# Sixty-four-column products set among the gate/up products, and products behind the last expert, in an encoder layer kernel

## What is computed

```python
def expert_choice_ffn(h, w_router, w_gate, w_up, w_down):
    n = B * L
    cap = max(1, EC_FACTOR * n // N_EXPERTS)      # 64 of the prompt, 128 of the sample
    hf = h.reshape(n, D)
    aff = jax.nn.softmax((hf @ w_router).astype(jnp.float32), axis=-1)
    g, idx = lax.top_k(aff.T, cap)
    xe = hf[idx]
    hid = jax.nn.silu(jnp.einsum('ecd,edf->ecf', xe, w_gate)) * jnp.einsum('ecd,edf->ecf', xe, w_up)
    ye = jnp.einsum('ecf,efd->ecd', hid, w_down) * g[..., None].astype(h.dtype)
    y = jnp.zeros((n, D), h.dtype).at[idx.reshape(-1)].add(ye.reshape(-1, D))
```

## Time and profile before

| | before |
|---|---|
| median of 3 runs | 3176.76 us (3174.6, 3176.76, 3177.8) |
| span of the profiled execution, first to last instruction | 3174.2 us |
| mean granted TensorE clock | 0.995 |
| PE busy | 3117.6 us (98%), 19002 products |
| PEld busy | 2799.1 us (88%) |
| DVE busy | 2304.2 us (73%) |
| ACT busy | 1907.7 us (60%) |
| HBM read | 650.35 MB |

### The profile page before, as it was taken

The page is one execution under the profiler, slowest core; times in us unless marked ns, Lnnn a source line. Parts: engine busy times, 40 slices in busy tenths (PEclk is TensorE's granted clock), DMA queues, the critical chain, the costliest instruction groups (busy, mean ns, idle before and its releaser), DMA issues.

```text
span 3174.2 us, 49405 instructions
## 1 busy us (share of the span) xinstructions
PE 3117.6 (98%) x19002; PEld 2799.1 (88%) x19002; DVE 2304.2 (73%) x3555; ACT 1907.7 (60%) x3129; POOL 187.8 (6%) x191
## 2 busy tenths in 40 slices
PE   7999999998999999999999999999999999999998
PEld 5777766787999999999999999999999999999997
DVE  6789848458777767777777777777777776777775
ACT  6244478444666666656666666666666666665664
POOL 0000000001010101010101001010101010101000
PEclk9999999999999999999999999999999999999999
DMA  9321266437575747575766666675757574757562
GB/s 345 126 77 57 79 218 224 146 112 282 200 283 199 284 183 289 212 281 211 257 232 258 231 246 241 237 259 212 262 199 282 199 286 185 288 213 282 208 250 93
DMA packets 140941, 692.78 MB, mean 218 GB/s; under 512 B 11040, under 2 KB 48432, under 8 KB 116912
## 3 DMA queue, kind: packets, MB, share of 16 engines
q1 hardware_dynamic: 131680, 663.55, 56.1%
q0 software_dynamic: 8128, 25.17, 3.2%
q10 hardware_dynamic: 912, 1.00, 0.2%
HBM read 650.35 MB, written 39.34 MB: 217 GB/s over the span
## 4 chain that ended last, share of the span: by engine, by line
PE 76%; DVE 1%; DMA 0%; issue 0%; POOL 0%; ACT 0%; POOLq 0%; DVEq 0%
PE psG L1902 35%; PE psG L1904 16%; PE psY L1921 5%; PE psY L1924 5%; PE psY L1922 5%; PE psY L1923 5%; PE psY L1925 5%; DVE idxu L1362 0%; DVE affT L1365 0%; DVE vals L1359 0%; DMA xg<-xhat_d,iall 0%; PE psY L1840 0%; POOL out L1967 0%; DVE yp L2173 0%; DVE ye L2167 0%
## 5 line engine op out<-in xcount | busy, mean ns | idle before, releaser
L1902 PE MATMUL psG<-xe,w_gu_hi_part 128*128 128x384 f32 x5632 | 1617.2, 358 | 0.0
L1904 PE MATMUL psG<-xe,w_gu_lo_part 128*128 128x192 f32 x5632 | 1410.3, 250 | 0.0
L1904 PEld LDWEIGHTS psG<-xe,w_gu_lo_part 128*128 128x128 f32 x5632 | 1074.7, 191 | 13.1
L1902 PEld LDWEIGHTS psG<-xe,w_gu_hi_part 128*128 128x128 f32 x5632 | 1057.4, 188 | 13.8 <-DVE xe L2233 0.4
L2148 DVE TENSOR_TENSOR w_gu_lo_part<-raw_gu,w_gu_hi_part 128x1024 fp32r<-128x1024 f32 x704 | 859.9, 1223 | 119.3 <-ACT w_gu_hi_part L2026 119.3
L2026 ACT ACTIVATE w_gu_hi_part<-raw_gu 128x1024 fp32r<-128x1024 f32 x704 | 739.4, 1053 | 9.9 <-DMA raw_gu<-in_w_gu 9.9
L2054 ACT ACTIVATE low<-psG 128x384 f32<-128x384 f32 x352 | 172.8, 491 | 690.6 <-PE psG L1904 690.6
L2183 DVE TENSOR_TENSOR gu<-psG,low 128x384 f32<-128x384 f32 x352 | 195.9, 557 | 489.2 <-ACT low L2054 486.4
L2153 DVE TENSOR_TENSOR w_dn_lo_part<-raw_dn,w_dn_hi_part 128x1024 fp32r<-128x1024 f32 x352 | 431.0, 1224 | 1.6 <-ACT w_dn_hi_part L2037 1.3
L2037 ACT ACTIVATE w_dn_hi_part<-raw_dn 128x1024 fp32r<-128x1024 f32 x352 | 368.0, 1045 | 3.6 <-PE psY L1925 3.6
L1921 PE MATMUL psY<-w_dn_hi_part,hs 128*128 128x512 f32 x704 | 282.6, 401 | 0.0
(11 more groups left out here) (230 smaller groups left out, 3040.5 us busy)
## 6 DMA issues: line engine op xcount, KB each, us to landing
raw_gu<-in_w_gu SPq DMA_DIRECT2D x176, 2048.0 KB, 8.3
raw_dn<-in_w_down SPq DMA_DIRECT2D x176, 1024.0 KB, 9.3
shared<-in_ada_w SPq DMA_DIRECT2D x8, 2048.0 KB, 8.8
w_raw<-in_w_in SPq DMA_DIRECT2D x20, 512.0 KB, 5.3
bias<-in_bias SPq DMA_DIRECT2D x6, 1536.0 KB, 14.7
shared<-in_ada_pairs SPq DMA_DIRECT2D x4, 2048.0 KB, 16.5
qk_d<-shared SPq DMA_DIRECT2D x8, 768.0 KB, 3.8
qk<-qk_d SPq DMA_DIRECT2D x8, 768.0 KB, 7.3
```

The source lines that it names most:

```text
L1902: pe.matmul(bank[:, 0:2 * CAP], wh, xe[:, k, :, :].rearrange("p a b -> p (a b)"), start=(k == 0), stop=False, skip_group_check=True)
L1904: mm = pe.matmul(bank[:, 0:CAP], wl, xe[:, k, 0, :], start=False, stop=(k == KD - 1), skip_group_check=True)
```

## The change

It has these parts, all in the tensor engine's block of `experts`:

1. Each `pp` x low weights product (128 stationary columns: prompt high and low parts) is replaced by `small_down`, whose stationary operand is the 64 columns of the prompt's high parts alone and whose result goes to rows 0 to 63 of the same bank. The low x low rows are no longer computed.
2. For the downs of steps 1 to 17 of each expert, the two `small_down` products (one per half) are issued in the `gate_up` that stands ahead of that `down`, among its up products (m = 1): one behind the slice k = 4, one behind k = 6. `gate_up` there waits for `dn_lo` and `hid_lo`, and the `down` no longer does. For the steps 0 and 18 to 21 they stay in `down`.
3. Behind the loop over the experts come 36 products into `psG` (192, 256, 384 and 512 moving columns with 128 stationary columns, 192 and 512 with 64 stationary columns, six of each), behind a wait for `gu_sum`; then a wait for `y_scaled` at its final count, and 18 products whose operands have 64 partitions, in alternating halves.
4. The loop over the experts stands in the new text twice: once ahead of these products (added lines) and once behind them (the lines that were there).

```diff
@@ -1742,6 +1742,8 @@
+    SMALL_AT = (4, 6)
+
@@ -1884,7 +1886,8 @@
-                def gate_up(e, i, first, last):
+                def gate_up(e, i, first, last, ahead=None):
+
                     a = i % 2
                     n = e * FT + i
@@ -1903,12 +1906,23 @@
                             mm = pe.matmul(bank[:, 0:CAP], wl, xe[:, k, 0, :], start=False, stop=(k == KD - 1),
                                            skip_group_check=True)
+                            if ahead is not None and m == 1 and k in SMALL_AT:
+                                if k == SMALL_AT[0]:
+                                    pe.wait_ge(dn_lo, e * FT + ahead + 1)
+                                    pe.wait_ge(hid_lo, e * FT + ahead + 1)
+                                small_down(ahead, SMALL_AT.index(k), False)
                     mm.then_inc(gu_done, 1)
 
-                def down(e, i, first):
+                def small_down(i, h, last):
+
+                    return pe.matmul(psY[0:CAP_P, 2 + h, :], hs[:, i % HS, P:CAP], d_lo[:, i % DS, h * 512:(h + 1) * 512],
+                                     start=False, stop=last, skip_group_check=True)
+
+                def down(e, i, first, ahead):
                     n = e * FT + i
-                    pe.wait_ge(dn_lo, n + 1)
-                    pe.wait_ge(hid_lo, n + 1)
+                    if not ahead:
+                        pe.wait_ge(dn_lo, n + 1)
+                        pe.wait_ge(hid_lo, n + 1)
                     if i == 0:
                         if first:
                             pe.wait_ge(merged, 7)
@@ -1921,20 +1935,38 @@
                         pe.matmul(psY[:, h, :], s_hi, wh, start=st, stop=False)
                         pe.matmul(psY[:, h, :], s_hi, wl, start=False, stop=False)
                         pe.matmul(psY[:, h, :], s_lo, wh, start=False, stop=en)
-                        pe.matmul(psY[:, 2 + h, :], pp, wh, start=st, stop=False)
-                        mm = pe.matmul(psY[:, 2 + h, :], pp, wl, start=False, stop=en)
+                        mm = pe.matmul(psY[:, 2 + h, :], pp, wh, start=st, stop=en, skip_group_check=True)
+                        if not ahead:
+                            mm = small_down(i, h, en)
                     mm.then_inc(dn_done, 1)
 
                 def expert(e, first, last):
                     for i in range(FT - 2):
-                        gate_up(e, i, first, last)
+
+                        ahead = i - BEHIND if i > BEHIND else None
+                        gate_up(e, i, first, last, ahead)
                         if i >= BEHIND:
-                            down(e, i - BEHIND, first)
+                            down(e, i - BEHIND, first, ahead is not None)
 
                     gate_up(e, FT - 2, first, last)
                     gate_up(e, FT - 1, first, last)
                     for i in range(FT - 2 - BEHIND, FT):
-                        down(e, i, first)
+                        down(e, i, first, False)
+                for e in range(EXPERTS):
+                    expert(e, e == 0, e == EXPERTS - 1)
+
+                pe.wait_ge(gu_sum, EXPERTS * FT)
+                w = w_hi[:, 0, 0, :]
+                for columns, rows in ((192, P), (256, P), (384, P), (512, P), (192, 64), (512, 64)):
+                    for i in range(6):
+                        pe.matmul(psG[0:rows, i % 2, 0:columns], w[:, i * P:i * P + rows],
+                                  xe[:, i % 2:i % 2 + 2, :, :].rearrange("p k a b -> p (k a b)")[:, 0:columns], start=True, stop=True)
+                pe.wait_ge(y_scaled, 4 * EXPERTS)
+                for half, columns in ((0, 384), (1, 192), (0, 192), (1, 384)) * 3 + ((0, 512), (1, 512)) * 3:
+                    at = slice(64 * half, 64 * half + 64)
+                    pe.matmul(psG[:, half, 0:columns], w[at, 0:P],
+                              xe[at, 0:2, :, :].rearrange("p k a b -> p (k a b)")[:, 0:columns], start=True, stop=True)
+
                 for e in range(EXPERTS):
                     expert(e, e == 0, e == EXPERTS - 1)
 
```

## The result

The changed kernel takes 5572.11 us (median of 4 runs, 5571.8 to 5573.01) against 3176.76 us: the ratio is 1.754 (95% interval 1.752 to 1.757). The forecast was 5553, range 5536 to 5594. The profiled execution took 5573.01 us at a span of 5571.2 us.

The account below looks back on a forecast made before the run. PE's unbroken string of products bounds the expert stage. First pass's end 3145.6, fillers 8.7, second pass 2411.8 - 0.3 - 16.5, end 0.2 + 1.0 give span 5550.5; plus 2.6, 5553 us, range 5536 to 5594.

Parts of the forecast that it names:

- The second loop: PE's repeated expert loop: nothing stops or shortens it, costing one pass more, 2411.8 us less about 0.3 us.
- the bound of a faster pass for PE alone: Second pass: down slots could fall from 0.231 to 0.2265 us with PE alone, 10 us less.
- The 0.3 us that the second pass was to save at the first expert: Second pass: no cost for the first expert's arrival in four parts, about 0.3 us less.
- the end is PE's: End of execution: PE's work sets it; the rival, end not PE's, gave 3160 us, chance 0.03.
- The fillers: The 54 products between the passes: 5.8 plus 2.9, together 8.7 us on the path; 7.3 if halves overlap, 13 if stalled.
- The moved wait: Wait for dn_lo in gate_up(i + 2): costs nothing, some 12.4 us available against 5.8 us needed.
- The rival of the stall: Small products: a narrow stationary operand stalls the array, 216 us a pass, 6018 us in all; chance 0.15.
- The small products: 544 a pass moved among gate/up products: 0.030 us saved each, 16.5 us a pass, 33 us in both.
- Inserting costs 0.2265 + 0.17 - 0.198 = 0.1985 us: Moved small product behind 192 columns in gate_up: its load hides wholly; 0.2265 to 0.231 us leaves the down.
- The 160 that stay save nothing: Small products kept in their down: no saving, since their 128-column load is already behind 512 columns.
- the load gives nothing: Rival, moved small products: they cost what they did, 33 us more, 5586 us, or rather 5578; chance 0.11.
- The sum: Whole span: first pass, fillers, second pass and end give 5550.5 us; plus 2.6 us median over span, 5553 us.

Follow-up runs that it names:

- kernel before run twice: Kernel before with PE's expert loop a second time behind a wait for the last scaled result, no narrow or added products: 5583.07 us.
- quarters: Changed kernel without second loop and products behind it, each small product cut into two of 256 moving columns, behind slices 0, 2, 4, 6: 3159.07 us (0.9948).
- Two edits: Changed kernel without second loop and 54 products: small products moved at 128 stationary columns, 3174.70 us (0.9994); or 64 columns but unmoved, 3174.88 us (0.9995).

## Why the prediction was right, and which term was off

**The second loop**: right. It was read as one pass more at the pace of the first, 2411.5 without the saving. The kernel before run twice shows 2413.2, of which 1.7 are the clock behind the pause; the bound of a faster pass for PE alone (10 us) did not come: 2405.9 against 2405.8 in the changed kernel. The 0.3 us that the second pass was to save at the first expert did not show in the sum, since that expert's gate/up pairs ran at 290 ns there in place of 284.4. That the end is PE's is shown by taking the loop out: 3170 us.

**The fillers**: 7.6 us on the path for 8.7 forecast (7.3 to 13 were the bounds). The first 36 took the 5.8 of the forecast; the 18 half-height ones took 1.8 in place of 2.9, since neighbours in opposite halves overlap (some start 4 ns apart). Without the second loop they are hidden, as the prediction said. They hold the clock, but cost more than the pause and the lower clock did in the kernel before run twice (5.7).

**The moved wait**: PE never waited at it, as forecast. The slack has an end: with steps 18 and 19 moved too, PE waited ahead of step 21.

**The rival of the stall** fell for float32r: in turn with wide products a narrow one has its 230 ns. By the Trainium skill, "PSUM — Partial Sum Buffer", The four PSUM rules, float32r takes the full column group; the runs with 64 stationary columns agree. The Trainium skill, "TensorEngine Tiling (Array Packing)", Key Properties, has a change of tiling mode drain the engine; the plain float32 product's 0.34 us a turn agree with that.

**The small products** were mis-sized: 16.5 us a pass forecast, 6.0 measured. Two steps of the prediction failed.

The first is "Inserting costs 0.2265 + 0.17 - 0.198 = 0.1985 us". A gate_up with two small products takes 4950.8 ns where one without takes 4525.9. Of the difference, 4.1 belong to the 384-column product behind the down (175.0 in place of 170.9); the rest is 210.4 for each insertion, mostly since the small product's slot is 234.6 and not 226.5, and that of the 384 behind it 174.6 and not 170. The other side of this step was right: ten products of a down and the 384 behind took 2505.0 ns, eight and the 384 take 2050.8, so 227.1 each, within the 226.5 to 231 of the forecast. That is 16.7 ns saved in place of 30, and 544 x 16.7 = 9.1 us (544 x 30 ns is 16.3, not 16.5). A step takes 6.83 us, where 6.79 was the forecast's sign and 6.86 that of no saving.

The second is "The 160 that stay save nothing": they cost. The last four downs of an expert take 9250.3 ns in place of 9102.5, and the step 0 takes 6882.1 in place of 6842.5: in 16 experts 3.0 us, which leaves 6.0. From the fourth product on, those downs had 226.7 ns a product; with narrow ones among them it is 225.8 to 236.

The rival "the load gives nothing" fell too: with the full width at the same places 1.8 of the 6.0 us are left, and in quarters the half load is worth 27.0 us a pass. But the time alone would not have told: 5572 lies nearer to this rival's 5578 than to the 5553 of the forecast. The mechanism held, since a small product has 234.6 ns where a wide one in its place has 252.9. What was wrong was to read slots as constants of a shape: a product of 512 columns has 224 to 236 ns by the order around it.

**The sum**: span 5571.2 for 5550.5. 21.0 from the small products in two passes, 1.1 since the stage began later (751.47), -1.1 from the fillers, -0.8 at the end (0.4 us behind the last slot in place of 1.2), 0.4 since the second pass was no shorter than the first: 20.6. The median lies 0.9 above the profiled span, not 2.6, so 19 us remain. Against 5553 an error of 19 us is small because one term, the second pass of 2406 us, is nearly all of the change; of the small products' 33 us, 21 did not come.

The time hangs on two lines that repeat a loop. Without them the changed kernel would be 0.2% faster than before, and with its small products in quarters 0.5%.

## What to carry to other kernels

In a stream of matrix products that never waits, look for the products whose moving side is shorter than the next load; what stands behind such a product should have the smallest load. Measure the whole period of the stream (here a step, 6860.0 ns) and not the one slot that was changed, since its neighbours' slots shift with it. Cut what can fill such places as finely as its own slot still hides the load behind it (256 moving columns did, at 122 ns or less against a load of 0.11 us). Read a diff of generated program order for repeated calls: counts that only grow let a second pass run without an error or a wait, at full price.

## What was not expected of the hardware

The same series of products with the same operands ran at 487 or at 500 ns a turn, by what had run ahead of it (eleven series in one execution). Gate/up pairs, with no small product near, have two values as well: 284.4 ns nearly everywhere, 290 in the first expert of the changed kernel's second pass, and 290 in the first two gate_ups of every expert with quarters. Two edits that shorten a step by 6.7 and by 12.6 ns shorten it by 33.3 together. That part of this is the same effect is likely, since the downs of all these kernels have different slots for the same products (224 to 236 ns), but no run here separates it. And a pause of 3.9 us ahead of a stream that had run for milliseconds was followed by a granted clock of 0.72 over 6 us.
